# Low halves of weight blocks on GpSimd around two sparse attentions, and roots, spreads and output blocks in another order

## The reference

```python
y_a = dsa_mixer(rms_norm_2(dq...), rms_norm_2(dk, ...), dv, iq, ik, iw)   # keeps the top 256 keys of an index score
y_b = nsa_mixer(rms_norm_2(nq...), kc, vc, ks, vs, kw, vw, sigmoid(ng), ...)  # compressed + 4 selected blocks + window
y_c = ssd_mixer(...)
gates = jax.nn.sigmoid(mg.reshape(bsz, seq, 3, D_MODEL))
mix = (gates[:, :, 0] * (y_a @ w_br_dsa[l]) + gates[:, :, 1] * (y_b @ w_br_nsa[l])
       + gates[:, :, 2] * (y_c @ w_br_ssd[l]))
```

## Time and profile before

| | us |
|---|---|
| median of 3 runs | 2971.26 (2971.16 to 2973.33) |
| the profiled execution, run time | 2973.71 |
| the profiled execution, span of its trace | 2971.9 |
| PE busy in that span | 2771.3 (93%) |
| DVE, ACT, POOL busy | 1631.5 (55%), 1135.3 (38%), 73.3 (2%) |
| mean granted TensorE clock | 0.960 |

### The profile page before, as it was taken

The page is one execution under the profiler, slowest core; times in us unless marked ns, Lnnn a source line. Parts: engine busy times, 40 slices in busy tenths (PEclk is TensorE's granted clock), DMA queues, the critical chain, the costliest instruction groups (busy, mean ns, idle before and its releaser), DMA issues.

```text
span 2971.9 us, 38479 instructions
## 1 busy us (share of the span) xinstructions
PE 2771.3 (93%) x13807; PEld 2227.5 (75%) x13807; DVE 1631.5 (55%) x2981; ACT 1135.3 (38%) x1860; POOL 73.3 (2%) x84
## 2 busy tenths in 40 slices
PE   7999999989999999998988997989899988999998
PEld 5567888878888788887765885667677777778887
DVE  5335726446554662634866337753677766464452
ACT  4343322225553422222437324852355543232221
POOL 0000000000000000000000000000011110000000
PEclk9999999979999999997999988999899998999999
DMA  3112333212111233232120220002222222323331
GB/s 136 42 57 71 114 94 97 99 36 79 56 56 36 85 108 98 93 99 71 57 71 1 83 81 29 1 22 92 72 70 71 64 67 69 121 92 100 95 102 64
DMA packets 60079, 219.33 MB, mean 74 GB/s; under 512 B 6448, under 2 KB 6576, under 8 KB 59824
## 3 DMA queue, kind: packets, MB, share of 16 engines
q1 hardware_dynamic: 58352, 211.33, 22.5%
q0 software_dynamic: 1600, 6.29, 0.6%
HBM read 213.41 MB, written 4.19 MB: 73 GB/s over the span
## 4 chain that ended last, share of the span: by engine, by line
PE 79%; DVE 10%; ACT 5%; issue 3%; DVEq 3%; ACTq 0%; DMA 0%; POOL 0%; SPq 0%
PE ps L366 22%; PE ps L368 22%; PE ps L367 22%; PE ps L447 1%; PE ps L500 1%; DVE big L2965 1%; PE ps L1788 1%; DVE ring_lo L306 1%; DVEq L3018 1%; PE ps L751 1%; PE ps L1331 1%; PE ps L455 1%; DVE work L1862 1%; ACT ring_hi L299 1%; PE ps L1769 1%
## 5 line engine op out<-in xcount | busy, mean ns | idle before, releaser
L366 PE MATMUL ps<-a_hi,ring_hi 128*128 128x512 f32 x1960 | 790.6, 403 | 57.0 <-DVE ring_lo L306 30.8
L368 PE MATMUL ps<-a_hi,ring_lo 128*128 128x512 f32 x1960 | 776.1, 396 | 0.0
L306 DVE TENSOR_TENSOR ring_lo<-ring,ring_hi 128x1024 fp32r<-128x1024 f32 x381 | 466.1, 1225 | 555.0 <-ACT ring_hi L299 523.8
L367 PE MATMUL ps<-a_lo,ring_hi 128*128 128x512 f32 x1896 | 750.5, 396 | 0.0
L299 ACT ACTIVATE ring_hi<-ring 128x1024 fp32r<-128x1024 f32 x381 | 400.7, 1055 | 526.1 <-PE ps L368 524.0
L366 PEld LDWEIGHTS ps<-a_hi,ring_hi 128*128 128x128 f32 x1960 | 376.4, 192 | 141.9 <-issue 28.1
L368 PEld LDWEIGHTS ps<-a_hi,ring_lo 128*128 128x128 f32 x1960 | 375.9, 192 | 81.3
L367 PEld LDWEIGHTS ps<-a_lo,ring_hi 128*128 128x128 f32 x1896 | 364.3, 192 | 75.1 <-issue 1.2
L367 PE MATMUL ps<-hid_lo,ring_hi 128*128 128x512 f32 x960 | 375.5, 391 | 0.0
L366 PE MATMUL ps<-hid_hi,ring_hi 128*128 128x512 f32 x896 | 349.7, 390 | 5.6 <-DVEq L1067 5.6
L368 PE MATMUL ps<-hid_hi,ring_lo 128*128 128x512 f32 x896 | 349.2, 390 | 0.0
(11 more groups left out here) (395 smaller groups left out, 3240.8 us busy)
## 6 DMA issues: line engine op xcount, KB each, us to landing
ring<-weights SPq DMA_DIRECT2D x395, 512.0 KB, 3.5
h<-x SPq DMA_DIRECT2D x1, 2048.0 KB, 10.0
residual<-h POOLq DMA_DIRECT2D x2, 1024.0 KB, 4.8
h<-residual POOLq DMA_DIRECT2D x1, 2048.0 KB, 11.2
out<-h POOLq DMA_DIRECT2D x1, 2048.0 KB, 7.6
tab<-tables SPq DMA_DIRECT2D x1, 1648.0 KB, 16.1
big<-positions SPq DMA_DIRECT2D x1, 256.0 KB, 3.4
col<-columns SPq DMA_DIRECT2D x1, 164.5 KB, 4.2
```

Source lines behind the costliest of these rows:

```text
L306: dve.tensor_tensor(lo, M.ring[:, b % RING, :], hi.bitcast(F32), ALU.subtract).then_inc(M.sem("blocks_split"), 1)
L366: pe.matmul(out, w_hi, hi, start=start, stop=False)
L367: pe.matmul(out, w_hi, lo, start=False, stop=False)
L368: return pe.matmul(out, w_lo, hi, start=False, stop=stop)
```

## The change

1. **DSA.** GpSimd takes the low halves of 14 blocks, `dsa_in`+8 to +21; `TOPK_RESTS` is gone and DVE's 48 rounds stand uninterrupted. The reciprocal stands behind them. Four spreads stand ahead of tile 21, five behind it, none ahead of tile 19.
2. **NSA.** GpSimd takes the low halves of `dsa_out`+4 to +7 (`nsa_pool`), 18 blocks with the above. The first two of `nsa_out` stay with DVE, but behind the pair attention. All 11 spreads stand in a row behind branch 1; branches 2 and 3 stand behind the quads; `turned(n)` and the branches alternate in another order. ACT does its four exponentials ahead of rounding `dsa_out`+4. The ranking's masks of group 0 stand ahead of branch 7 on DVE.
3. **`weigh`** multiplies `cmp_seen` into the 128x16 reciprocals and no longer into the 128x512 probabilities.
4. **`nsa_out`** is laid out as gate, gate, output, output, and the loops of PE, ACT and DVE follow.

```diff
-def branch_out_pe(pe, M, name, y_hi, y_lo, per_tile, unroll, wait_y):
+def branch_out_pe(pe, M, name, y_hi, y_lo, wait_y):
...
+    with pe.Fori(0, NT // 2) as i:
+        for n in range(4):
+            u, out = n % 2, n // 2
+            if not out:
+                pe.wait_ge(M.sem(f"{name}_free"), i * 2 + (u + 1))
+            b = FIRST[name] + n
+            wait_split(pe, M, b, i, 4)
+            if out:
+                wait_y()
+            hi, lo = (y_hi, y_lo) if out else (M.a_hi, M.a2_lo)
...
+def branch_out_act(act, M, name):
+    with act.Fori(0, NT // 2) as i:
+        for u in range(2):
...
+            round_block(act, M, FIRST[name] + u + 2, i, 4)
+        for u in range(2):
+            round_block(act, M, FIRST[name] + u + 4, i, 4)
...
+    with dve.Fori(0, NT // 2) as i:
+        for u in range(2):
+            rest_block(dve, M, FIRST[name] + u + 2, i, 4)
+        for u in range(2):
...
+            rest_block(dve, M, FIRST[name] + u + 4, i, 4)
...
-TOPK_RESTS = (7, 12, 17, 21, 25, 28, 32, 35, 38, 41, 43, 46)
...
         project(t)
         if 7 <= t < 16:
             head_total_pe(pe, M, "dsa_norm", t - 7)
-        if t == 18:
-            spread(0)
-            spread(1)
         if t == 20:
-            for k in range(2, 5):
+            for k in range(4):
                 spread(k)
-    for k in range(5, 9):
+    for k in range(4, 9):
         spread(k)
...
-            if n in TOPK_RESTS:
-                rest_block(dve, M, FIRST["dsa_in"] + 8 + TOPK_RESTS.index(n))
-            if n == 40:
-                dve.wait_ge(M.sem("norm_root"), 1 + M.past("dsa_norm", "root"))
-                dve.reciprocal(M.inv[:, 0:72], M.root[:, 0:72]).then_inc(M.sem("norm_inverse"), 1)
...
+    pool.wait_ge(M.sem("blocks_split"), splits_before(FIRST["dsa_in"] + 8))
+    for t in range(8, 14 + NT):
+        rest_block(pool, M, FIRST["dsa_in"] + t)
     R.pairs.stage_pool(pool, M, "dsa_norm", 1, 9)
...
+def nsa_pool(pool, M):
+    pool.wait_ge(M.sem("blocks_split"), splits_before(FIRST["dsa_out"] + 4))
+    for n in range(4, NT):
+        rest_block(pool, M, FIRST["dsa_out"] + n)
+    pool.wait_ge(M.sem("nsa_cmp_kept"), 4)
...
     first_branch(1)
-    for k in range(4):
-        spread(k)
-    first_branch(2)
-    for k in range(4, 8):
-        spread(k)
-    first_branch(3)
-    for k in range(8, 11):
+    for k in range(11):
         spread(k)
...
-    for u in range(4, NT):
-        first_branch(u)
-        if u >= 5:
-            turned(u - 5)
+    first_branch(2)
+    first_branch(3)
+    turned(0)
+    first_branch(4)
+    turned(1)
+    turned(2)
+    first_branch(5)
     turned(3)
+    first_branch(6)
+    first_branch(7)
...
+        dve.tensor_tensor(heads(R.top), heads(R.top), M.t("cmp_seen", P)[:, 0:P:32].unsqueeze(1).broadcast_to([P, 4, QT]),
+                          ALU.mult)
+        dve.drain()
         dve.tensor_tensor(rows16(p), rows16(p), wide(R.top), ALU.mult)
-        dve.drain()
-        dve.tensor_tensor(heads(p), heads(p), four(M.t("cmp_seen", P)), ALU.mult)
...
     R.pairs.dve(dve, M, gate)
-    branch_out_dve(dve, M, "nsa_out", 1, 2, lambda: split_y_dve(dve, M, "nsa", R.y))
+    dve.wait_ge(M.sem("blocks_split"), splits_before(FIRST["nsa_out"]))
+    rest(8)
+    rest(9)
+    branch_out_dve(dve, M, "nsa_out", lambda: split_y_dve(dve, M, "nsa", R.y))
```

126 lines of the change are left out of this document (45 added, 81 removed).

## The result

The changed kernel takes 2942.3 us (median of four runs, 2940.86 to 2942.54) against 2971.2 for the kernel before (four runs, 2969.38 to 2973.33): a ratio of 0.99, 95% interval 0.9885 to 0.9915, or 28.9 us less. The direction was forecast, the size was not. Its profiled execution took 2940.86 us.

What follows compares the result with a forecast made beforehand. PE, busy 93% of the span, was taken to bound the kernel, so time could come only from its waits or lower clock. DSA 9.0, NSA 7.5 and outputs 4.5 summed to 21.0 us: 2950, range 2944 to 2960.

Steps and rivals of the forecast that it cites:

- DSA: Selection stretch: first scores start at 1540.7 in place of 1549.83, gain 9.0 us, bounds 7 and 9.3.
- The bound of 2.45 us of holds for each low half: DSA selection: GpSimd may hold DVE up to 2.45 us for each of ten low halves, losing at most 2 us.
- NSA: Stretch up to the second attention's first mask: quads begin earlier, gain 7.5 us after holds and clock loss, 13.5 without.
- The three holds of 1.5: NSA: GpSimd's low halves of branches 4, 5 and 6 each hold DVE's products 1.5 us, 4.5 us in all.
- branch 2: NSA: branch 2 done 19.4 us after the quads start, from 24.9 us less one block of 5.5.
- The clock term of 1.5: NSA: PE's lower clock behind a wait for `weigh` costs another 1.5 us.
- Outputs: Output blocks: the second gate block fills PE's wait of 5.56 us, leaving 1.6; gain 4.5 us, between 4.0 and 5.6.
- Rival A: No hold in NSA and no clock loss: 28 us gained in all, 2943; chance 0.15.
- Rival D: GpSimd's low half takes 5.5 us, PE waits in DSA: slower than before, 2981, deciding from about 4.8 us; chance 0.05.
- B: NSA stretch gives nothing, from lower clock in spreads and quads and DVE held in every `weigh`: 2958; chance 0.2.
- C: GpSimd's low half takes 4 us, six DSA blocks late by 0.5, longer holds: 8 us gained, 2963; chance 0.06.

Runs made afterwards that it cites:

- the kernel with the order alone: Kernel before with the DSA part's order (reciprocal behind the 48 rounds, first spreads later), all low halves left to DVE: 2959.5 us, ratio 0.9964.
- the kernel with DVE's own low halves: Changed kernel with the low halves of dsa_out blocks 4 to 7 back on DVE, none on GpSimd in NSA: 2938.5 us, ratio 0.9901.
- The doubled low halves: Changed kernel with each of GpSimd's 14 low halves in the DSA selection computed twice, same result: 2953.1 us.

## Why the prediction was wrong in size

**DSA: right.** Forecast 9.0, measured 9.2. GpSimd's low half took 2.41 us (2.45 taken), no norm, spread or block waited for one, and the selection ended at 1499.87. The bound of 2.45 us of holds for each low half did not show at all: DVE's operations of the selection read one wide tensor, and none was lengthened. But "GpSimd" was the wrong owner of the gain, as the kernel with the order alone shows: my sum took DVE's low halves out of its order before it moved the reciprocal, and only the second step was needed.

**NSA: right in mechanism, mis-sized.** Forecast 7.5, measured 10.0 (8.5 in the second profile). The quads came 10.5 us earlier (10.3 forecast). Two terms failed. The three holds of 1.5 were 1.57, 0.21 and 0.92, 2.7 us together, since only the first low half met its product early. And branch 2 was done 17.7 us after the start of the quads, where the sum had 19.4. PE's waits were 1.28 and 3.97. The clock term of 1.5 stood up in this profile: from `turned(2)`, behind the longer wait, to the end of branch 5 PE took 7.3 us, and 6.0 for `turned(0)` and branch 4. In the second profile the same piece took 8.8, which is the other value of this stretch. The sum had no fourth hold. It was there, 2.1 us beside the low half of branch 7, and cost little: in the kernel with DVE's own low halves the whole stretch is only 0.7 us shorter.

The Trainium skill's page SBUF — State Buffer, section Who interferes with whom, says that a VectorE instruction with two SBUF inputs contends with a GpSimd instruction that reads SBUF, and that the one which comes second waits for the whole of the other. The trace agrees: the narrow product took 1.75 us, to the end of GpSimd's 2.41. The Trainium skill's page GPSIMD Engine Reference, section Engine selection, would leave such work on VectorE, GpSimd being some two times slower. The low half agrees, 2.41 us against 1.23; the kernel without GpSimd's low halves takes the same time within what can be measured.

**Outputs: right, the better of two values.** Forecast 4.5 between 4.0 and 5.6, measured 5.5. The wait was 1.47 (1.6 forecast), and the clock was 1.00 over the whole stage.

**The sum: the step that failed.** The three terms came to 24.7 instead of 21.0, which alone would have given 2971.3 - 24.7 = 2946.6 from the median shown ahead of the prediction, inside the range. The other 5.2 us are the pair and the input stage, for which the sum had no term at all: it took unedited stages as unchanged. They went from 80.1 and 102.9 us to 78.0 and 99.8, in both profiles of the changed kernel and in nine more kernels with its order of the DSA stretch; why these stages follow what lies ahead of them stays open. Rival A's 2943 was near the result, but by another way: it had holds and clock loss at nothing, and both were there.

**Rival D: its price was wrong.** The doubled low halves show 0.5 us of wait for each block where the same working gave 1.2. The point from which it decides was set too early too: at 4.8 us a low half the stretch still takes 109.0, 5 us less than before.

**Rivals B and C** did not occur: NSA gave its gain although its clock was lowered (0.92), and the low half took 2.41 us.

## What to carry to other kernels

When an engine waits inside a long order of small steps, first ask what stands needlessly behind that wait. Here one reciprocal of 0.6 us and the spreads that need it, put elsewhere, gave 8.9 of the 9.2 us of their stretch, and 14 low halves on another engine added next to nothing. On a kernel that PE bounds, cut two profiles at the same instructions and compare the unedited stages too: here they held a sixth of the gain. Profile one kernel twice before a difference between kernels is read: two stages repeated to the hundredth, two others moved by 1.6 us. Parts of a change may be worth more together than their sum, so measure them in combination before one is dropped.
